# Third layer of a fused transformer block: recurrence and convolution issued among the key and value blocks instead of behind them

## The chip, the cores and the metric

The kernel runs on one core of one Trainium2 chip. The core has five engines with a queue of instructions each: TensorE (PE, matrix products; its weight loads are shown as PEld), VectorE (DVE), ScalarE (ACT), GpSimd (POOL) and SyncE (SP, which issues transfers). They meet only at semaphores. The metric is the device time of one execution in microseconds (us).

## What is computed

Four layers on 256 rows of 1024 words, all float32. The first two are attention layers, the last two a second model with key and value projections of a memory. What the change touches is the mixer of the third layer: a gated recurrence over chunks of 32 positions (four heads of 128) beside a causal depthwise convolution with 31 taps over 512 channels, followed by a layer norm and SiLU.

```python
def hgrn2_chunked(q, k, v, log_f):          # S_t = diag(f_t) S_{t-1} + k_t v_t^T, o_t = S_t^T q_t
    b = jnp.cumsum(log_f, axis=3)
    b_last = b[:, :, :, -1:, :]
    q_t = q * jnp.exp(b)
    k_t = k * jnp.exp(-b)
    scores = jnp.where(causal, jnp.einsum('bhntd,bhnsd->bhnts', q_t, k_t), 0.0)
    o_intra = jnp.einsum('bhnts,bhnsv->bhntv', scores, v)
    k_end = k * jnp.exp(b_last - b)
    d_state = jnp.einsum('bhnsd,bhnsv->bhndv', k_end, v)
    decay = jnp.exp(b_last[:, :, :, 0, :])
    ...
    return o_intra + jnp.einsum('bhntd,bhndv->bhntv', q_t, s_start)

def hybrid_ab_mixer(x, w_in, lb, hg_norm_g, cv_w, cv_b, cv_ln_g, cv_ln_b, w_out):
    q, f_pre, i_v, g, a, a_gate = jnp.split(x @ w_in, ...)
    f = lb + (1.0 - lb) * jax.nn.sigmoid(f_pre)
    k = (1.0 - lb) * jax.nn.sigmoid(-f_pre)
    o = hgrn2_chunked(q, k, i_v, jnp.log(f))
    o = o * lax.rsqrt(jnp.mean(jnp.square(o), axis=-1) + RMS_EPS) * hg_norm_g * jax.nn.silu(g)
    u = causal_depthwise_conv_31(a * jax.nn.sigmoid(a_gate), cv_w) + cv_b
    u = jax.nn.silu(layer_norm(u, cv_ln_g, cv_ln_b))
    return jnp.concatenate([o, u], axis=-1) @ w_out
```

## The kernel before, in words

**Blocks.** Every weight matrix is streamed in blocks of 1 MB (a "unit" in the code). Projections have K8 units: eight 128-row tiles of a 256-column strip; output matrices have DN units of two 128-row tiles of 1024 columns. A float32 product is made of three matmuls on a high and a low part of each operand (`passes`, L496 to L498). For each unit SyncE loads `w_raw`, which has two slots (`load`, L373, waiting for the low part of the unit two before); ScalarE copies each half to `w_hi` (`hi`, L1061, which waits for the load and for TensorE to be through with that half of the unit two before); VectorE subtracts to make `w_lo` (`lo`, L1568); TensorE waits for `lo_done` of the half it starts (`k8_unit`). So preparation runs two units ahead. After a unit ScalarE evacuates its bank in `step`, between the two high parts. A K8 unit alternates between banks 0 and 1.

**Order in the third layer** (list `PHASES`). `ab_t`, eight units: two of the convolution's input (HA), two of its gate (HG), two of the forget gate (SF and its complement SN), two of the query (HQ). `ab_nat`, four: value (HV) and output gate (GG). `xk0` and `xv0`, four each: keys and values of the cross attention that follows, from the memory; they don't depend on this layer. Then the recurrence and convolution, then `ab_out`, four DN units. Within the layer the order on every engine is written out by hand.

On VectorE the projections' stretch holds, between low parts (`stream`), the product for the convolution (UP, L2118), taps (`taps`, L2137: four operations of 128x256, one for each 128 channels, and a wait for the engine's own last step before each group), the softmax of the lower bound (L2107 to L2150), forget gate (L2155), scans (L2166), decayed keys and queries (L2178 to L2183). ScalarE makes the logarithm (L1417) and exponentials (L1420 to L1425).

**Behind the last value unit** TensorE waits for its evacuation, then does the first of six convolution taps as products with a diagonal (L935; ScalarE makes the diagonals in two buffers, L1436), turns the keys (L945), makes the scores (L950) and for seven chunks a state product (L960) and one more tap. VectorE masks the scores, updates the state after each product (L2207) and does a tap between. TensorE makes the outputs (L969, L977); then follow the sum of the convolution, the norm of the output (squares L2220, power on GpSimd, scale L2236), mean (L984) and variance (L988) of the convolution over channels by a product with ones, square root (L1451), reciprocal, SiLU (L1455), turning of the output (L994), and the splits into high and low parts (L2247, L2253). `down_phase("ab_out")` waits for all of that.

## Time and profile before

| | before |
|---|---|
| median of 3 runs | 1414.07 us (1413.47 to 1415.58) |
| profiled execution | 1414.13 us, its span 1412.3 us |
| PE busy | 1334.1 us, 94% |
| DVE busy | 856.0 us, 61% |
| ACT busy | 661.9 us, 47% |
| mean granted clock of PE | 0.967 of full speed |

Times in rows are us from the start of the span. A row of the timeline has start, duration, engine, line, operation, written tile <- read tiles, count of merged instructions, and in brackets the idle time of the engine before it with what ended it. The duration of merged instructions runs from the first start to the last end. The chain of waits lists what the end of the program followed from, each piece with its own share.

### The profile page before, as it was taken

Reading aid. Unit: us, or ns where it says so; the run is one execution under the profiler, and the core shown is the slowest. Engines: PE = TensorE matmul, PEld = TensorE weight load, DVE = VectorE, ACT = ScalarE, POOL = GpSimd, SP = SyncE. Lnnn points to the kernel's source line nnn. Section 1 sums busy time; section 2 is a strip of 40 time slices with the busy share of each in tenths; the row PEclk is TensorE's granted clock in tenths of the full one; section 3 lists DMA queues with packets and bytes.
Section 4 is the critical chain, followed back from the end, with each engine's and each line's share of the span. In section 5 each row is a group of like instructions: output and inputs, shape, how many; then the busy total and the mean of one; then the engine's idle time right before and its main releaser. Section 6 shows DMA issues by size and latency. Waiting matters only on the chain.

```text
span 1412.3 us, 23518 instructions
## 1 busy us (share of the span) xinstructions
PE 1334.1 (94%) x9430; PEld 1249.4 (88%) x9430; DVE 856.0 (61%) x1162; ACT 661.9 (47%) x1004; POOL 61.6 (4%) x72
## 2 busy tenths in 40 slices
PE   6999998999999998989996989899999999899996
PEld 6999997889998897889985888899999898799995
DVE  6566676665764444658896545655555755655555
ACT  5445676454447666345642343443433354334341
POOL 0012011000110000000000000100000000000000
PEclk9999999999999999989998999899999999899998
DMA  7555532445533332645540353665555344365552
GB/s 236 180 178 181 171 124 93 140 160 179 179 121 123 116 120 80 218 149 179 182 154 0 120 178 120 216 208 180 179 188 195 123 153 145 124 195 189 178 181 86
DMA packets 167923, 219.68 MB, mean 156 GB/s; under 512 B 3691, under 2 KB 151478, under 8 KB 167846
## 3 DMA queue, kind: packets, MB, share of 16 engines
q1 hardware_dynamic: 164502, 206.68, 45.0%
q0 software_dynamic: 3040, 11.20, 2.5%
q8 instruction: 54, 0.88, 0.3%
q10 hardware_dynamic: 304, 0.73, 0.1%
q14 instruction: 23, 0.19, 0.0%
HBM read 217.54 MB, written 1.05 MB: 155 GB/s over the span
## 4 chain that ended last, share of the span: by engine, by line
PE 83%; DVE 9%; ACT 3%; DMA 3%; issue 2%; POOL 0%; DVEq 0%; SPq 0%; ACTq 0%
PE bank L496 24%; PE bank L497 23%; PE bank L498 23%; DVE w_lo L1568 2%; PE bank L745 2%; DVE small L1592 1%; DVE h L1709 1%; PE bank L705 1%; ACT w_hi L1061 1%; PE bank L724 1%; PE bank L935 1%; DVE att L1630 1%; PE bank L757 1%; DMA w_raw<-in_o_w_out 1%; DMA w_raw<-in_e_w_mem_kv 1%
## 5 line engine op out<-in xcount | busy, mean ns | idle before, releaser
L1568 DVE TENSOR_TENSOR w_lo<-w_raw,w_hi 128x1024 fp32r<-128x1024 f32 x388 | 471.9, 1224 | 395.9 <-ACT w_hi L1061 392.5
L1061 ACT ACTIVATE w_hi<-w_raw 128x1024 fp32r<-128x1024 f32 x388 | 409.3, 1058 | 469.6 <-PE bank L498 372.5
L496 PE MATMUL bank<-u_hi,w_hi 128*128 128x256 f32 x1088 | 314.6, 289 | 3.3 <-DVE u_lo L1690 3.3
L497 PE MATMUL bank<-u_lo,w_hi 128*128 128x256 f32 x1088 | 311.6, 286 | 0.0
L498 PE MATMUL bank<-u_hi,w_lo 128*128 128x256 f32 x1088 | 311.4, 286 | 0.0
L496 PE MATMUL bank<-w_hi,y_hi 128*128 128x512 f32 (+1 forms) x656 | 235.1, 358 | 11.1 <-issue 7.6
L496 PE MATMUL bank<-w_hi,u_hi 128*128 128x256 f32 x832 | 237.9, 286 | 0.0
L497 PE MATMUL bank<-w_lo,u_hi 128*128 128x256 f32 x832 | 236.2, 284 | 0.0
L498 PE MATMUL bank<-w_hi,u_lo 128*128 128x256 f32 x832 | 236.1, 284 | 0.0
L497 PE MATMUL bank<-w_lo,y_hi 128*128 128x512 f32 (+1 forms) x656 | 231.6, 353 | 0.0
L498 PE MATMUL bank<-w_hi,y_lo 128*128 128x512 f32 (+1 forms) x656 | 231.2, 352 | 0.0
L496 PEld LDWEIGHTS bank<-u_hi,w_hi 128*128 128x128 f32 x1088 | 212.7, 196 | 6.0 <-DVE u_lo L1690 5.1
L497 PEld LDWEIGHTS bank<-u_lo,w_hi 128*128 128x128 f32 x1088 | 212.8, 196 | 0.9
L498 PEld LDWEIGHTS bank<-u_hi,w_lo 128*128 128x128 f32 x1088 | 212.6, 195 | 0.0
L497 PEld LDWEIGHTS bank<-w_lo,u_hi 128*128 128x128 f32 x832 | 160.5, 193 | 0.0
L496 PEld LDWEIGHTS bank<-w_hi,u_hi 128*128 128x128 f32 x832 | 160.5, 193 | 0.0
L498 PEld LDWEIGHTS bank<-w_hi,u_lo 128*128 128x128 f32 x832 | 160.4, 193 | 0.0
L496 PEld LDWEIGHTS bank<-w_hi,y_hi 128*128 128x128 f32 x656 | 127.4, 194 | 26.9 <-issue 9.2
L498 PEld LDWEIGHTS bank<-w_hi,y_lo 128*128 128x128 f32 x656 | 127.1, 194 | 16.2
L497 PEld LDWEIGHTS bank<-w_lo,y_hi 128*128 128x128 f32 x656 | 127.5, 194 | 14.7
L1492 POOL TENSOR_TENSOR pow_out<-pow_in,mhalf 128x1 f32<-128x1 f32 (+5 forms) x27 | 38.8, 1436 | 988.8 <-DVEq L1562 988.8
L1083 ACT ACTIVATE nat<-bank 128x512 f32<-128x512 f32 (+1 forms) x70 | 41.6, 594 | 66.5 <-PE bank L498 66.4
(277 smaller groups left out, 1323.4 us busy)
## 6 DMA issues: line engine op xcount, KB each, us to landing
w_raw<-in_e_w_in SPq DMA_DIRECT2D x28, 1024.0 KB, 5.1
w_raw<-in_o_w_in SPq DMA_DIRECT2D x28, 1024.0 KB, 5.2
w_raw<-in_ffn_wg SPq DMA_DIRECT2D x22, 1024.0 KB, 5.3
w_raw<-in_ffn_wu SPq DMA_DIRECT2D x22, 1024.0 KB, 5.3
w_raw<-in_ffn_wd SPq DMA_DIRECT2D x22, 1024.0 KB, 5.0
w_raw<-in_ab_w_in SPq DMA_DIRECT2D x12, 1024.0 KB, 5.2
w_raw<-in_e_w_out SPq DMA_DIRECT2D x8, 1024.0 KB, 4.9
w_raw<-in_o_w_out SPq DMA_DIRECT2D x8, 1024.0 KB, 5.1
```

Of the source, the lines that this page charges most:

```text
L496: pe.matmul(out_ap, ah, bh, start=start, stop=False, skip_group_check=True)
L497: pe.matmul(out_ap, ah, bl, start=False, stop=False, skip_group_check=True)
L498: return pe.matmul(out_ap, al, bh, start=False, stop=stop_, skip_group_check=True)
L705: mm = pe.matmul(bank[SC[pr]][:, SEQ * m:SEQ * m + SEQ], XQT[:, 2 * hd + j, P * m:P * m + P], (KT2 if g < 32 else KT1)[:, 2 * hd + j, :], ...
L724: mm = pe.transpose(bank[PTB][:, dst:dst + P], s[:, src:src + P], ident)
L745: mm = pe.matmul(o[:, w * m:w * m + w], p[:, SEQ * k + P * m:SEQ * k + P * m + P], v[:, k, cs], start=(k == 0), stop=(k == 1))
L757: mm = pe.transpose(bank[YTB][:, SEQ * j + P * m:SEQ * j + P * m + P], ys[g % 2][:, w * m + P * j:w * m + P * j + P], ident)
L935: mm = pe.matmul(bank[f // 2][:, SEQ * (f % 2):SEQ * (f % 2) + SEQ], DIAG[i % 2][:, P * f:P * f + P], UP[:, f, k:k + SEQ], start=(i == 0 a ...
L1061: act.activation(w_hi[:, at:at + 1024], w_raw[:, at:at + 1024], ACT.Copy).then_inc(hi_done, 1)
L1083: act.activation(dst(col), two(bank[b][:, :], SEQ), func).then_inc(evacuated, 1)
L1492: pool.tensor_tensor(pow_out[:, at:at + w], pow_in[:, at:at + w], mhalf[:, 0:w], ALU.pow)\
L1568: v.tensor_tensor(w_lo[:, at:at + 1024], w_raw[:, at:at + 1024], w_hi[:, at:at + 1024].bitcast(F32), ALU.subtract).then_inc(lo_done, 1)
```

## The change

Recurrence, convolution and norms of the third layer are issued inside and between the units of `ab_nat`, `xk0` and `xv0` (helper `among` calls `k8_unit` with `between`, a piece of work between the two halves of a unit). Part by part:

- SyncE: the first four units are ordered convolution input 0, gate 0, input 1, gate 1; ScalarE evacuates them in that order. UP is made in two halves, and taps run in two groups of 256 channels (`taps(g, n)`: n taps of group g, two operations each, and each operation waits only for the last one of its own 128 channels).
- Six taps on TensorE become two (CV_PE 6 to 2); both diagonals are made at once, both taps are done at once after state product 5. VectorE has 29 taps in place of 25.
- TensorE: keys turned within unit 1 of `ab_nat`, scores behind it, state products 0 to 6 within and behind units 2, 3 of `ab_nat` and 0, 1 of `xk0`, outputs within units 1 and 2 of `xk0`, output turned within unit 0 of `xv0`, mean within unit 2 and variance within unit 3 of `xv0`. The output phase starts its first two units when the recurrence's part is split (`hg_yl`), the other two when the convolution's part is (`conv_lo`).
- VectorE: the same steps in a new order, with single low parts (`lo_of`) between them. `two_ahead(u)` makes the two halves of unit u + 2.
- ScalarE: the forget gate's scale and shift go into the logarithm (four activations of 128x256 with scale and bias), and the key's scale is four copies of 128x256 on ScalarE; the operations of VectorE for these go. The decayed products are made in the order LF, KT, HQ.
- The softmax of the lower bound moves to the first layer's `e_kv` phase: VectorE does it before the memory keys' norm, ScalarE its exponential before the stream of `e_nat`.
- Mean, variance and the turned output use other banks (6, 7, 2 and 3).

The diff, cut to its core:

```diff
-CV_PE = 6
-PE_FIRST = 1
+CV_PE = 2
...
-            u = k8(UNIT0["ab_t"], w, 2048, 4)
+            u = UNIT0["ab_t"]
+            for j in range(2):
+                u = k8(u, w, 2048 + SEQ * j, 1)
+                u = k8(u, w, 2560 + SEQ * j, 1)
...
-            k8_phase("ab_nat", uh, ul, False)
-            pe.wait_ge(tL, turned("mem2"))
-            k8_phase("xk0", yh_[:, 8:16, :], yl_[:, 8:16, :], True)
-            k8_phase("xv0", yh_[:, 8:16, :], yl_[:, 8:16, :], False)
-            pe.wait_ge(up_ready, 1)
-            pe.wait_ge(evacuated, BANK0["xv0"] + 4)
...
+            def among(phase, j, between=None):
+
+                u, kb = UNIT0[phase] + j, BANK0[phase] + j
+                xh, xl = (uh, ul) if phase == "ab_nat" else (yh_[:, 8:16, :], yl_[:, 8:16, :])
+                k8_unit(u % 2, kb % 2, xh, xl, phase == "xk0", 2 * u + 1, kb - 1, between=between)
...
+            pe.wait_ge(tL, turned("mem2"))
+            among("ab_nat", 0)
+            among("ab_nat", 1, key_turn)
+            chunk_scores()
+            among("ab_nat", 2, lambda: state_part(0))
+            state_part(1)
+            among("ab_nat", 3, lambda: state_part(2))
+            state_part(3)
+            pe.wait_ge(up_ready, 2)
+            pe.wait_ge(hg_sm, 2)
+            among("xk0", 0, lambda: state_part(4))
+            state_part(5)
+            for i in range(CV_PE):
+                conv_tap(i)
+            among("xk0", 1, state_and_out)
+            among("xk0", 2, lambda: chunk_out(1))
+            among("xk0", 3)
+            among("xv0", 0, out_turn)
+            among("xv0", 1)
+            among("xv0", 2, conv_mean)
+            among("xv0", 3, conv_var)
             pe.wait_ge(hg_yl, 1)
+            down_phase("ab_out", 0, 2)
             pe.wait_ge(conv_lo, 2)
-            down_phase("ab_out")
+            down_phase("ab_out", 2)
...
+            act.wait_ge(lb_sub, 1)
+            act.activation(lbe, lbe, ACT.Exp).then_inc(lb_exp, 1)
             stream("e_nat", 0, 4, nat_dst(eQ))
...
-            act.activation(LF, LF, ACT.Ln).then_inc(hg_ln, 1)
-            stream("xk0", 0, 2, t_dst(KT2))
+            act.wait_ge(evacuated, BANK0["ab_t"] + 6)
+            for f in range(4):
+                ins = act.activation(LF[:, f, :], SF[:, f, :], ACT.Ln, scale=oml[:, f:f + 1], bias=lb[:, f:f + 1])
+            ins.then_inc(hg_ln, 1)
+            step(UNIT0["ab_t"] + 6, copy_out(t_dst(HQ), 0), BANK0["ab_t"] + 6)
             act.wait_ge(hg_b, 1)
             act.activation(SF, HB, ACT.Exp)
             act.activation(KT, HB, ACT.Exp, scale=-1.0)
...
+            for f in range(4):
+                ins = act.activation(SN[:, f, :], SN[:, f, :], ACT.Copy, scale=oml[:, f:f + 1])
             act.wait_ge(hg_b, 2)
             act.activation(LF, LF, ACT.Exp).then_inc(hg_e, 1)
...
+                            v.wait_ge(dve_step, tap_step[f])
                             mark(v.scalar_tensor_tensor(CA[:, f, :], UP[:, f, k:k + SEQ], ws, CA[:, f, :],
                                                         ALU.mult, ALU.add))
...
+            mark(v.memset(UP, 0.0))
+            up(0)
+            taps(0, 2)
+            two_ahead(tu + 2, lambda: taps(0, 2))
+            taps(0, 1)
+            two_ahead(tu + 3, lambda: taps(0, 2))
+            up(1)
+            two_ahead(tu + 4, lambda: taps(1, 2))
+            taps(1, 2)
+            two_ahead(tu + 5, lambda: taps(1, 2))
+            taps(1, 2)
+            scans()
+            two_ahead(tu + 6, lambda: taps(1, 1))
+            taps(0, 1)
+            decayed()
+            two_ahead(tu + 7)
+            taps(1, 2)
+            two_ahead(nu, lambda: taps(0, 2))
+            taps(1, 2)
+            two_ahead(nu + 1, lambda: taps(0, 1))
+            masked_scores()
+            state(0)
...
+            state(6)
+            two_ahead(ku + 1, lambda: taps(0, 3), lambda: taps(1, 3))
+            two_ahead(ku + 2, lambda: taps(0, 4), lambda: taps(1, 3))
+            out_squares()
+            lo_of(ku + 5, 0)
+            out_norm()
+            lo_of(ku + 5, 1)
+            taps(0, 2)
+            two_ahead(vu, lambda: taps(1, 4))
+            taps(0, 2)
+            lo_of(vu + 3, 0)
+            y_low()
+            taps(0, CV_K)
+            lo_of(vu + 3, 1)
+            taps(1, CV_K)
+            conv_sum()
+            lo_of(vu + 4, 0)
             v.wait_ge(cv_mu, 1)
```

`tu`, `nu`, `ku`, `vu` are the first units of `ab_t`, `ab_nat`, `xk0`, `xv0`. Between `state(0)` and `state(6)` VectorE alternates: half a low part, two taps of a group, the next state; `gate_scale` and one tap stand before `state(6)`.

## Rows read from the trace of the kernel before

**Rows 1.** The page: engines' busy time; loads (last: us to landing).

```profile
PE 1334.1 (94%) x9430; PEld 1249.4 (88%) x9430; DVE 856.0 (61%) x1162; ACT 661.9 (47%) x1004; POOL 61.6 (4%) x72
...
w_raw<-in_ab_w_in SPq DMA_DIRECT2D x12, 1024.0 KB, 5.2
```

**Rows 2.** By stretch: length; busy PE, PEld, DVE, ACT, POOL; clock; DMA.

```profile
680.00:727.70 47.70, 47.01 (x392) 46.81 (x391) 41.60 (x62) 27.81 (x33) 0.00 (x0) 1.00 0.56 188
727.70:777.00 49.30, 35.05 (x224) 29.23 (x224) 35.48 (x72) 16.73 (x39) 2.77 (x3) 0.89 0.08 29
```

**Rows 3.** The chain of waits, start of the output phase.

```profile
777.33 0.76 PE bank L496
...
778.10 0.43 PE bank L497
...
788.92 0.23 PE bank L498
```

**Rows 4.** Timeline of TensorE behind the last value block.

```profile
726.73 0.28 PE L498 MATMUL bank<-w_hi,y_lo 128*128 128x256 f32 x1
...
730.02 1.97 PE L935 MATMUL bank<-att 128*128 128x256 f32 x8 [3.00 <-ACT att L1436]
731.82 1.03 PE L945 MATMUL bank<-cst,nat 128*128 128x128 f32 x8
732.69 1.95 PE L950 MATMUL bank<-nat 128*128 128x128 f32 x16
...
749.62 1.71 PE L960 MATMUL bank<-nat 32*128 32x128 f32 x16
...
751.25 1.16 PE L969 MATMUL bank<-nat 128*128 128x128 f32 x8
...
754.26 1.16 PE L969 MATMUL bank<-nat 128*128 128x128 f32 x8
...
757.75 1.99 PE L984 MATMUL bank<-att,ones 128*128 128x256 f32 x8
```

**Rows 5.** Timeline of VectorE in the third layer; the taps' line (mean ns).

```profile
625.07 1.23 DVE L1568 TENSOR_TENSOR w_lo<-w_raw,w_hi 128x1024 fp32r<-128x1024 f32 x1
...
645.28 1.67 DVE L2137 SCALAR_TENSOR_TENSOR att<-att,gT 128x256 f32<-128x256 f32 x4
...
649.62 3.38 DVE L2137 SCALAR_TENSOR_TENSOR att<-att,gT 128x256 f32<-128x256 f32 x8
...
684.92 2.44 DVE L2166 TENSOR_TENSOR_SCAN nat<-cst,nat 128x256 f32<-128x256 f32 x4 [1.15 <-ACT nat L1417]
...
688.88 2.36 DVE L1568 TENSOR_TENSOR w_lo<-w_raw,w_hi 128x1024 fp32r<-128x1024 f32 x2
...
738.77 1.12 DVE L2207 SCALAR_TENSOR_TENSOR nat<-nat,small,bank 128x128 f32<-128x128 f32 x4 [0.62 <-PE bank L960]
...
758.48 1.23 DVE L2220 TENSOR_TENSOR nat<-nat 128x1024 f32<-128x1024 f32 x1 [4.13 <-ACT nat L1449]
...
L2137 DVE SCALAR_TENSOR_TENSOR att<-att,gT 128x256 f32<-128x256 f32 x96 | 40.1, 481 | 0.3
```

**Rows 6.** ScalarE: block 8's evacuation; two forms (busy, mean ns).

```profile
663.69 0.60 ACT L1083 ACTIVATE nat<-bank 128x512 f32<-128x512 f32 x1 [1.74 <-PE bank L498]
...
L1204 ACT ACT_TABLE_LOAD x7 | 9.0, 1283 | 0.1
...
L1204 ACT ACTIVATE att<-att,small 128x256 f32<-128x256 f32 x12 | 6.0, 496 | 0.0
```

**Rows 7.** Timeline of VectorE: the lower bound's last steps.

```profile
664.65 0.17 DVE L2150 TENSOR_SCALAR small<-small 128x4 f32<-128x4 f32 x1
```

**Rows 8.** Timelines of VectorE and ScalarE in the first layer.

```profile
52.75 3.50 DVE L1568 TENSOR_TENSOR w_lo<-w_raw,w_hi 128x1024 fp32r<-128x1024 f32 x3 [0.32 <-DVE nat L1666]
...
55.13 0.60 ACT L1083 ACTIVATE nat<-bank 128x512 f32 x1 [1.93 <-PE bank L498]
```

**Rows 9.** Timeline of TensorE before the third layer.

```profile
602.68 1.97 PE L604 MATMUL bank<-cst,h 128*128 128x128 f32 x8 [2.80 <-DVEq L2095]
```

More of the change, by code:

```diff
@@ L952, in _, with conv_tap @@
-            mm.then_inc(hg_st, 1)
-            pe.wait_ge(hg_kn, 1)
-            for n in range(N_CHUNK - 1):
+            def conv_tap(i):
+                pe.wait_ge(diag_ready, i + 1)
+                k = CV_K - CV_PE + i
+                for f in range(4):
+                    mm = pe.matmul(bank[4 + f // 2][:, SEQ * (f % 2):SEQ * (f % 2) + SEQ],
+                                   DIAG[i % 2][:, P * f:P * f + P], UP[:, f, k:k + SEQ],
+                                   start=(i == 0 and f % 2 == 0), stop=(i == CV_PE - 1), skip_group_check=True)
+                mm.then_inc(diag_used, 1)
@@ L996, in _, with out_turn, conv_mean @@
-            mm.then_inc(hg_yt, 1)
+            def out_turn():
+                pe.wait_ge(hg_y, 1)
+                for f in range(4):
+                    for m in range(2):
+                        mm = pe.transpose(bank[2 + f // 2][:, SEQ * (f % 2) + P * m:SEQ * (f % 2) + P * m + P],
+                                          ON[:, m, P * f:P * f + P], ident)
+                mm.then_inc(hg_yt, 1)
+            def conv_mean():
+                pe.wait_ge(conv_ready, 2)
+                for f in range(4):
+                    mm = pe.matmul(bank[6][:, 0:SEQ], ones[:, :], CA[:, f, :], start=(f == 0), stop=(f == 3))
+                mm.then_inc(cv_mu, 1)
@@ new lines, in conv_var @@
+            def conv_var():
+                pe.wait_ge(cv_c, 2)
+                for f in range(4):
+                    mm = pe.matmul(bank[7][:, 0:SEQ], ones[:, :], CS[:, f, :], start=(f == 0), stop=(f == 3))
+                mm.then_inc(cv_var, 1)
+            def among(phase, j, between=None):
+                u, kb = UNIT0[phase] + j, BANK0[phase] + j
+                xh, xl = (uh, ul) if phase == "ab_nat" else (yh_[:, 8:16, :], yl_[:, 8:16, :])
+                k8_unit(u % 2, kb % 2, xh, xl, phase == "xk0", 2 * u + 1, kb - 1, between=between)
@@ L2194, in _, with two_ahead @@
-            v.wait_ge(hg_tr, 1)
-            for m in range(2):
-                v.tensor_tensor(STM[:, m, :].rearrange("p (a b) -> p a b", b=P),
-                                bank[4 + m][:, :].rearrange("p (a b) -> p a b", b=P), hm, ALU.mult).then_inc(hg_sm, 1)
-            for n in range(N_CHUNK - 1):
+                        tap_step[f] = steps[0]
+            def two_ahead(u, first=None, second=None):
+                lo_of(u + 2, 0)
+                if first is not None:
+                    first()
+                lo_of(u + 2, 1)
+                if second is not None:
+                    second()
@@ new lines, in _ @@
+            masked_scores()
+            state(0)
+            lo_of(nu + 4, 0)
+            taps(0, 2)
+            state(1)
+            lo_of(nu + 4, 1)
+            taps(1, 2)
+            state(2)
+            lo_of(nu + 5, 0)
+            taps(0, 2)
+            state(3)
+            lo_of(nu + 5, 1)
+            taps(1, 2)
+            state(4)
+            lo_of(ku + 2, 0)
+            taps(0, 2)
+            state(5)
+            lo_of(ku + 2, 1)
+            gate_scale()
+            taps(1, 1)
```

328 lines of the change are left out of this document (155 added, 173 removed).

## Prediction

> **What bounds the kernel now.** I read the page's busy shares first: TensorE is busy 94% of the span, so outside its pauses there is nothing to win. VectorE has 61% [rows 1]. Then the busy time of two stretches of the third layer: in the later half of the projections TensorE is full (47.01 of 47.70 us) and VectorE is busy 87%; in the next, which holds recurrence, convolution and norms with no projection beside them, the two share the time, 35 us each of 49.3, and the clock is 0.89 [rows 2]. So this layer is serial there. The chain of waits shows that the output phase's first matmul starts at 777.33 [rows 3]. TensorE's timeline shows where the stretch begins: its last value matmul starts at 726.73 and runs 0.28, so it ends at 727.0; a pause of 3.0 behind ScalarE's diagonals, then dense work of 27 us up to the mean at 757.75, and from VectorE's squares at 758.48 on a relay of short steps on three engines [rows 4, 5]. Hence 777.3 - 727.0 = 50.3 us without weight matmuls. After it the output phase begins at the lower clock, 1.2 GHz: a 128x512 matmul takes 0.43 of the chain at 778.10 against 0.23 at 788.92 [rows 3]. Thirteen such steps (to 783.2) lose 13 x 0.2 = 2.65 us.
>
> **What moves on TensorE.** Its records in that stretch price every item at full clock [rows 4]: key transposes 0.9, scores 1.8, seven state products, two in 1.63 (749.62 to 751.25) to 1.1 each with a wait (I take 1.0), a tap 1.95, outputs of the first four chunks 3.0 (751.25 to 754.26), of the last four 3.5 (to 757.75), a mean 1.9, a variance of the same eight matmuls as much, turning the output as much as the eight key transposes, 1.0. Six taps become two, so 4 x 1.95 = 7.8 us are gone. The rest is inserted: 0.9 + 1.8 + 7.0 + 3.9 + 6.5 + 3.8 + 1.0 = 24.9 us. If nothing waited, the last value block would end at 727.0 + 24.9 = 751.9, and the output phase start there: a gain of 25.4, with the clock 28.1 us. This is the floor.
>
> **What VectorE must do in that time.** Prices are start-to-start [rows 5]: a half block's low part 1.14 (two last 2.36, one 1.23), a large product as much or 1.25 with a wait, scans and subtraction 3.96 (684.92 to 688.88), a state 1.07, squares and sum 2.7 (two of 1.23, a small one and their waits), mean, difference and square 3.1 by the same count. A tap of four operations lasts 1.67 with single ones of 0.48, so they start 0.397 apart; eight last 3.38, so the first of a group, which waits for the last of the group before, starts 0.52 after it. The new taps run in pairs and wait for the operation two back, which has ended: I take 0.397 x 2 = 0.795 per pair-tap. 29 taps x 2 pairs = 58 x 0.795 = 46.1 us, against 25 x 1.71 = 42.8 before. Forget-gate scaling and key scaling (1.38 + 1.14) go to ScalarE. From the low part of block 4 to the sum of the convolution: 32 low parts 36.5, taps 46.1, zeroing and two products 2.4, scans 4.0, decayed products 3.6, scores 1.3, states 7.1, gate 1.2, squares 2.7, norm 2.5, low part of the output 1.2, sum 1.4: 110 us. Starting at 626.2 (the low part at 625.07 [rows 5]) this can't be done before 736.2, and the mean on TensorE needs it.
> The rows above have taps of 0.48 starting 0.397 apart without a wait and 0.52 with one [rows 5]. The Trainium skill, "VectorE: DVE Perf Modes", section "The DRAIN you can't avoid", says that the next operation does not start before the pipe has emptied (unless it is one that isn't held back) and that a semaphore between operations costs nothing extra. By that rule taps would start 0.48 apart, grouped or not, the tail below would end 26 x 0.083 = 2.2 us later and the time be 1400; I go by the rows.
>
> **The walk.** Number the blocks from 0 (eight of the first projection, four of the gate and value one, four keys, four values, then 20 to 23 output). Block 8 is evacuated at 663.69 now [rows 6], every block takes 5.76, and ScalarE's and VectorE's preparation of a block's half runs two blocks ahead of it.
> *Block 9.* ScalarE now makes the logarithm in four pieces of 128x256, then exponentials, then four scalings. A 128x256 one takes 0.50, four with overlap an estimated 1.6, and a table load 1.28 [rows 6]; a pass over 1024 words takes 1.05, 0.95 where the next follows. Block 5 is evacuated three blocks before 8, at 646.4; its two copies and the high part end at 648.45; table and logarithm at 651.4; scans on VectorE to 655.4; table and exponentials to 657.4; scalings 659.0; last exponential 660.05. VectorE's three products end at 663.65 (the last also waits for block 7's late evacuation, 661.6), and only then comes the low part of block 9, at 664.85. TensorE is ready at 663.5: it waits 1.4 us, a wait that the kernel now hasn't.
> *Blocks 9 to 14.* With the inserts TensorE ends them at 671.8, 680.4, 688.3, 696.3, 711.2, 720.5. At each of them VectorE has its state, low parts and taps done in time: for block 13 it is even through at 701.6 and waits until 705.3 for the last state product, and for ScalarE's copies until 712.8 and 722.0. A load takes 5.2 us from issue (page's median [rows 1]) and is issued when the low part two blocks before is made; all land before they are wanted.
> *From 722.0 on VectorE sets the time.* Seven low parts 8.0, 13 pair-taps 10.3, squares 2.7, norm with the power on GpSimd 2.9, output's low part 1.2, sum 1.4: 26.5, so the convolution's sum is there at 748.7. The norm is ready at 732.4 while TensorE stands in the middle of block 16 at 729.2: a wait of 3.2. The mean is wanted in the middle of block 18 at 744.9: a wait of 3.8. Behind it lie the mean 1.9, half a block 2.9, block 19 5.8 and the variance 1.9: the output phase starts at 761.2. The last convolution steps (square root, reciprocal, normalising, SiLU, split) then take from 758.4 to about 768, beside blocks 20 and 21, which need 10.9 us to 772: hidden, 4 us to spare.
> *The sum.* 777.3 - 761.2 = 16.1, plus 2.65 for the clock of the output phase. **Clock of the two new pauses:** before, the pause of 3.0 us to 730.02 left the clock high (a tap of 1.97 like all later ones), one of 2.8 before 602.68 did not: eight transposes took 1.97 there against 1.03 at 731.82 [rows 4, 9]. So a pause of 3 to 4 us may cost nothing or some 2.7 (the mean at 3.8 in place of 1.9 and a part of a half block). The first pause's loss would vanish in the second. I take 2.0.
> **Bound preparation moved forward.** The softmax of the lower bound (six small operations and an exponential) leaves this layer and stands before the first layer's key norm on VectorE. Its first two took 0.4, the four after the exponential 0.8, the last at 664.65 [rows 7]; with the exchange with ScalarE 1.6 us. There three low parts start at 52.75, the first ends at 53.98, and the block before the one that wants it is evacuated at 55.13, TensorE being free at 54.9 [rows 8]: 0.9 of the 1.6 is covered and 0.7 is not. Nearest bounds 0 and 1.6. The next load is late by as much, but its low part at 63.08 has 2 us to spare. ScalarE waits there until 47.1 in place of starting its copy at 46.38: nobody needs that copy before 52.75.
> Order of the first loads, half of the first product early, and the output phase in two calls: nothing, TensorE is full over all of them.
> In all 16.1 + 2.65 - 2.0 - 0.7 = 16.1 us. The profiled execution took 1414.13 (its span of 1412.3 and 1.8 around it), the median of the runs is 1414.07: **1398 us**.
>
> **Rivals.** *(a) TensorE stays the bound.* If VectorE's idle stretches near 703 to 722 fill, that is if ScalarE and the states come earlier than walked, both pauses (7.0) and block 9's 1.4 shrink: 1386 to 1391. For it: VectorE's bare work ends at 736. Against: the waits follow from the written order, and taps can't pass a state. 0.17.
> *(b) The preparation falls behind.* Low parts stand behind up to four taps (3.2 us) and behind states that wait for TensorE; each may make TensorE wait at blocks 9 to 17, where I found one wait. Six of 1 us and both clock losses (2.7 each): 1398 + 6 + 3 = 1407; range 1404 to 1411. For it: VectorE is at 87% already among the key and value blocks [rows 2]. 0.20.
> *(c) Slower.* The loop low part, load (5.2), copy, low part again closes around VectorE's queue: a late low part makes the next load late. Its price is one wait per block; it turns the balance when the twelve blocks 8 to 19 lose 16/12 = 1.35 us each beyond my walk; at 2 us each 1422. Against: 5.2 + 2.2 + 3.2 = 10.6 us of loop against 15.3 for two blocks. 0.03.
> *(d) The change doesn't overlap:* a semaphore of the recurrence always comes last, and TensorE stands inside a block as long as it stood behind them; only the four taps (7.8) are gained, and partly lost: about 1412, the same. 0.03.
>
> **Numbers.** Forecast 1391 to 1404: 0.57. With (a) 0.17, (b) 0.20, (c) 0.03, (d) 0.03. What this kernel's runs can tell from no change is about 0.2%, 2.8 us. Faster 0.93, same 0.04, slower 0.03. The range, 1388 to 1408, leaves out the ends of (a) and (b), with (c) and (d).
>
> **What would show it.** Between the last value matmul and the first output matmul no pause; the first output matmuls at 0.23; TensorE's waits in the layer: about 1.4 before block 9, 3 before turning the output, 4 before the mean, each behind VectorE; taps 0.397 apart; VectorE over 85% busy from 630 to 750; TensorE some 0.7 late near 55. Wrong: a mean without a wait (then rival a), waits on low parts in several blocks (b), a pause before the third output block on the convolution's split.

## The result and the profile after

The changed kernel takes 1399.05 us in the median of four runs (1398.35 to 1399.62), the kernel before 1413.77 beside it (1413.39 to 1415.58): a ratio of 0.9896, 95% interval 0.9881 to 0.991, 14.7 us less. The forecast was 1398. The profiled execution of the changed kernel has a span of 1397.8 us, 14.5 less than before, and a mean granted clock of 0.969.

Its page, the line of busy times, answers to [rows 1]: TensorE has 7.7 us less work (four taps gone), VectorE 3.2 more.

```profile
PE 1326.4 (95%) x9398; PEld 1244.5 (89%) x9398; DVE 859.2 (61%) x1171; ACT 656.6 (47%) x994; POOL 61.5 (4%) x72
```

**Where the time went.** GpSimd makes the powers of the norms ahead of the third layer and behind it, with the same code in both kernels, so its rows are good marks for the length of the layer. Timeline of GpSimd, kernel before (start, duration, line, operation, idle time ahead of it):

```profile
591.67 0.56 POOL L1492 TENSOR_TENSOR pow_out<-pow_in,mhalf 128x1 f32<-128x1 f32 x1 [1.29 <-DVEq L1562]
...
802.57 0.57 POOL L1492 TENSOR_TENSOR pow_out<-pow_in,mhalf 128x1 f32<-128x1 f32 x1 [25.80 <-DVEq L1562]
```

The same, kernel after:

```profile
594.10 0.55 POOL L1553 TENSOR_TENSOR pow_out<-pow_in,mhalf 128x1 f32<-128x1 f32 x1 [1.30 <-DVEq L1623]
...
788.11 0.57 POOL L1553 TENSOR_TENSOR pow_out<-pow_in,mhalf 128x1 f32<-128x1 f32 x1 [37.45 <-DVEq L1623]
```

The layer shrinks from 210.90 to 194.01 us, by 16.9. Of that 2.4 are lost before it begins (594.10 against 591.67), and behind it nothing moves: the second mark is 14.46 earlier, the span 14.5 shorter. "The layer" below is always the distance between these two marks; the times of the prediction's walk have to be read 2.4 later. Blocks are numbered as in the walk, and "the norm" and "the mean" stand for TensorE's turning of the output, which waits for the norm, and for its product that makes the convolution's mean.

The waits view of TensorE from 600 to 800, kernel after (who waited for whom: total us, times, longest):

```profile
PE bank L983 <- DVEq L1623: 3.6, 1, 3.6
PE bank L606 <- DVEq L2174: 2.8, 1, 2.8
PE bank L991 <- DVEq L1623: 2.3, 1, 2.3
PE bank L498 <- DVE w_lo L1629: 1.5, 1, 1.5
...
```

L606 is the turning of the input that [rows 9] shows before (2.80); two waits of 0.7 and 0.6 on the layer's input follow in the view. The other three are new and are the three pauses of the walk: ahead of turning the output (L983), of the mean (L991) and of block 9 (L498). The stretches in which they lie (length; busy PE, PEld, DVE, ACT, POOL; clock), kernel after:

```profile
680.00:727.70 47.70, 47.70 (x388) 44.99 (x388) 37.71 (x82) 15.98 (x19) 0.00 (x0) 1.00 0.34 111
727.70:755.00 27.30, 21.34 (x152) 20.78 (x151) 25.18 (x40) 9.05 (x12) 2.76 (x3) 0.87 0.50 158
755.00:765.00 10.00, 10.00 (x78) 9.74 (x77) 6.13 (x6) 4.36 (x5) 0.00 (x0) 1.00 0.50 181
```

Against [rows 2]: there TensorE was busy 35.05 of 49.30 us, with no weights to multiply. Now the stretch that holds the norm's and the mean's pause is 27.3 us with 21.3 busy, blocks of weights among them. There VectorE is busy 92% (25.18) and TensorE waits for it; in the ten us behind it TensorE is full.

The chain of waits, kernel after, where the output phase begins (the last matmul of 256 columns, then those of 512):

```profile
765.70 0.12 PE bank L500
765.82 0.23 PE bank L498
766.06 0.23 PE bank L499
```

It begins without a pause and at 2.4 GHz, where [rows 3] shows 0.43 a step.

### The profile page after: what moved, and what is told of

Its sections match the earlier page's. It is cut to its first block, busy times and chain, and to the rows that moved or that the text cites. A ratio compares the mean times of both kernels' runs of the same rounds, so it can differ in the third digit from the quotient of the medians.

```text
span 1397.8 us, 23384 instructions
## 1 busy us (share of the span) xinstructions
PE 1326.4 (95%) x9398; PEld 1244.5 (89%) x9398; DVE 859.2 (61%) x1171; ACT 656.6 (47%) x994; POOL 61.5 (4%) x72
## 3 DMA queue, kind: packets, MB, share of 16 engines
HBM read 217.54 MB, written 1.05 MB: 156 GB/s over the span
## 4 chain that ended last, share of the span: by engine, by line
PE 80%; DVE 11%; ACT 4%; DMA 3%; issue 2%; POOL 0%; DVEq 0%; SPq 0%; ACTq 0%
PE bank L498 23%; PE bank L499 23%; PE bank L500 23%; DVE w_lo L1629 3%; PE bank L747 2%; DVE small L1653 1%; ACT w_hi L1098 1%; DVE h L1770 1%; PE bank L707 1%; PE bank L726 1%; DVE att L1691 1%; PE bank L759 1%; DMA w_raw<-in_o_w_out 1%; DMA w_raw<-in_e_w_mem_kv 1%; PE bank L666 1%
## 5 line engine op out<-in xcount | busy, mean ns | idle before, releaser
L498 PE MATMUL bank<-u_hi,w_hi 128*128 128x256 f32 x1088 | 314.7, 289 | 3.3 <-DVE u_lo L1751 3.3
L498 PE MATMUL bank<-w_hi,u_hi 128*128 128x256 f32 x832 | 239.1, 287 | 2.2 <-DVE w_lo L1629 2.2
L498 PE MATMUL bank<-w_hi,y_hi 128*128 128x512 f32 (+1 forms) x656 | 235.3, 359 | 3.7 <-DVE w_lo L1629 3.7
L498 PEld LDWEIGHTS bank<-u_hi,w_hi 128*128 128x128 f32 x1088 | 213.0, 196 | 6.0 <-DVE u_lo L1751 5.1
L498 PEld LDWEIGHTS bank<-w_hi,u_hi 128*128 128x128 f32 x832 | 160.9, 193 | 3.0 <-DVE w_lo L1629 2.6
L498 PEld LDWEIGHTS bank<-w_hi,y_hi 128*128 128x128 f32 x656 | 127.8, 195 | 19.1 <-DVE w_lo L1629 3.0
L499 PEld LDWEIGHTS bank<-w_lo,y_hi 128*128 128x128 f32 x656 | 127.8, 195 | 14.5
```

Of the source, the lines that this page charges most:

```text
L498: pe.matmul(out_ap, ah, bh, start=start, stop=False, skip_group_check=True)
L499: pe.matmul(out_ap, ah, bl, start=False, stop=False, skip_group_check=True)
```

## The experiments

Theory A is the prediction's account, with the sizes of this trace: TensorE is full except in three pauses, each of which follows from a place in VectorE's written order; a pause can also halve the clock. The expectations name its rivals by letters. All twelve kernels start from the changed kernel unless said otherwise. A pair-tap is one tap of one group of 256 channels, two operations. The kernel before took 1415.54, 1413.83 and 1414.1 beside the three groups of runs (1415.54 beside norm_first, filled, block9_first and one_tap), and each ratio is to the one beside it, so across groups ratios or layers compare better than times.

### The order decides, not the work: norm_first, filled

```diff
-            two_ahead(ku + 2, lambda: taps(0, 4), lambda: taps(1, 3))
+            two_ahead(ku + 2, lambda: taps(0, 4))
             out_squares()
             lo_of(ku + 5, 0)
             out_norm()
             lo_of(ku + 5, 1)
+            taps(1, 3)
             taps(0, 2)
```

> The changed kernel with one edit on VectorE: the three taps of the second group that stood before the output's squares stand behind its norm. TensorE's pause before turning the output was 3.6 us with 3.5 us at the lower clock behind it, the pause before the mean 2.3 us. Theory A (from block 14 on VectorE's queue alone sets the end; its sum of work is unchanged): the first pause falls to about 1.2 us and its low clock goes, but the mean's pause grows by that to about 6 us and may lose the clock itself, so the output phase starts no earlier: 1398 to 1402 us. Rival B (each pause costs its own length): 2.4 us and the low clock's 1.9 us are won, 1395 us.

Measured 1400.34 (1398.3 to 1401.33), ratio 0.9898, 0.988 to 0.9917. Waits view of TensorE, 600 to 800:

```profile
PE bank L991 <- DVEq L1623: 6.2, 1, 6.2
...
PE bank L498 <- DVE w_lo L1629: 1.5, 1, 1.5
...
PE bank L983 <- DVEq L1623: 1.2, 1, 1.2
...
```

Three pair-taps moved behind the norm take 2.4 us off the norm's pause (3 x 0.79) and put 3.9 onto the mean's, since TensorE now comes to the mean earlier, without the pause's last 2.4 us and the 2.6 of lost clock behind it, while VectorE has as much to do as before and is there only 1.1 earlier. Nothing is won: both steps wait for one queue, and what is postponed falls due at the mean. The layer is 1.5 longer (195.48), for the mean now runs at half the clock, as its line shows (durations min/median/max in ns; 379 in the changed kernel):

```profile
L991 PE MATMUL bank<-att,ones x8: 634/634/795, 751.4 to 754.6; 128*128 128x256 f32 x8
```

The second kernel brings those three pair-taps forward instead, and three of the other group that stood between norm and mean, into VectorE's idle stretches before state 6 and behind it:

```diff
-            taps(1, 1)
+            taps(1, 4)
             state(6)
-            two_ahead(ku + 1, lambda: taps(0, 3), lambda: taps(1, 3))
-            two_ahead(ku + 2, lambda: taps(0, 4), lambda: taps(1, 3))
+            two_ahead(ku + 1, lambda: taps(0, 6), lambda: taps(1, 3))
+            two_ahead(ku + 2, lambda: taps(0, 4))
             out_squares()
             lo_of(ku + 5, 0)
             out_norm()
             lo_of(ku + 5, 1)
-            taps(0, 2)
```

> The changed kernel with six taps of a pair of channel blocks moved forward on VectorE into its two idle stretches: three before the last state, three before the wait for the high part of block 15's second half. Nothing is added or left out. Theory A (VectorE's queue behind block 14 sets the end): the norm is 2.4 us and the convolution's sum 4.8 us earlier, TensorE's first pause about 1 us at full clock, the mean's pause 1 to 2 us; 1394 us (1392.5 to 1396). Rival C (the pauses follow from TensorE's order and from ScalarE's copies, not from VectorE's work): no change, 1399 us.

Measured 1392.26 (1388.58 to 1397.66), ratio 0.9845, 0.9819 to 0.987; the layer takes 188.35, 5.7 less, of which 0.9 lies at its input, ahead of all that the edit touches (last section). The norm's pause is 1.2, and the transposes behind it run at full clock (272 ns). The idle time of VectorE before state 6 was 3.42 in the changed kernel and is 1.05 here (its timeline, behind the eight operations of four pair-taps):

```profile
702.83 3.25 DVE L2209 SCALAR_TENSOR_TENSOR att<-att,gT 128x256 f32<-128x256 f32 x8
707.12 1.12 DVE L2261 SCALAR_TENSOR_TENSOR nat<-nat,small,bank 128x128 f32<-128x128 f32 x4 [1.05 <-PE bank L957]
```

The mean's pause is 2.3 as in the changed kernel, and both edits leave 1.2 of the norm's. A expected the gain and about 1 us at the norm, the 3.6 less three pair-taps; C expected none. That no further tap can shorten this rest, A did not say.

### The floor under the pauses: taps_out

```diff
-                    if k >= CV_K - CV_PE:
+                    if k >= 15:
                         return
```

> The changed kernel with only 15 of the 29 taps on VectorE; 14 taps of both groups (28 x 0.8 = 22 us of VectorE) are left out, so the convolution's result is not the reference's. Nothing else is moved. Theory A: the pauses before the output's turning (3.6 and its low clock) and before the mean (2.3) go and block 9's 1.5 stays: 1391 us (1390 to 1392.5), no less, because behind them TensorE is full. Rival F (every us of VectorE's work stands on the path): 1399 - 22 = 1377 us. Rival C (the pauses have another cause): 1399 us.

Measured 1392.25 (1389.69 to 1393.54), ratio 0.9844, 0.9825 to 0.9862; layer 188.01. The kernel leaves out 28 pair-taps, 22 us of VectorE's work, and pauses of 1.5, 1.2 and 1.3 remain. A said that the norm's and the mean's would go: its time is met, its pauses are not. F, by which every us of VectorE counts (1377), is out. The timeline of VectorE shows what the pauses are made of:

```profile
736.32 1.23 DVE L1629 TENSOR_TENSOR w_lo<-w_raw,w_hi 128x1024 fp32r<-128x1024 f32 x1 [3.19 <-ACT w_hi L1098]
...
742.08 1.23 DVE L1629 TENSOR_TENSOR w_lo<-w_raw,w_hi 128x1024 fp32r<-128x1024 f32 x1 [0.88 <-ACT w_hi L1098]
743.23 1.28 DVE L2307 TENSOR_TENSOR att<-att,bank 128x512 f32<-128x512 f32 x2
```

and ScalarE's, where the copy that this low part needs follows the evacuation, and that the end of a block on TensorE:

```profile
740.51 0.60 ACT L1120 ACTIVATE mkv<-bank 128x512 f32<-128x512 f32 x1 [0.79 <-PE bank L500]
741.00 1.05 ACT L1098 ACTIVATE w_hi<-w_raw 128x1024 fp32r<-128x1024 f32 x1
```

The convolution's sum (L2307) stands in the queue behind a low part that can't start until the block ended on TensorE, 0.6 us of evacuation and 1.05 of copy are over: block end 740.5, low part 742.1 to 743.3, sum to 744.5, mean 744.6; but half a block is done on TensorE in 2.9. So TensorE waits 1.3 even if VectorE has nothing else to do. In filled the 2.3 are this floor, with one pair-tap (0.98) behind the same low part, which has waited 0.62 there. In the changed kernel that low part starts without a wait (749.96): the queue's work is later than the floor. Of its 3.6 and 2.3 the taps thus make 2.4 and 1.0, and 1.2 and 1.3 would remain without them. The norm's floor is of the same kind: in norm_first the squares start at 725.51, behind a low part at 724.37 that has waited 1.31 for its copy. Block 9 is no matter of taps either: its low part stands behind products that wait for ScalarE, not behind taps, and keeps its 1.5.

### Block 9: block9_first

```diff
             taps(0, 1)
+            lo_of(tu + 9, 0)
             decayed()
-            two_ahead(tu + 7)
+            lo_of(tu + 9, 1)
```

> The changed kernel with the low part of block 9's first half before the three decayed products on VectorE instead of behind them. It took TensorE 1.5 us of waiting at block 9 before. Theory A: TensorE's clock sets VectorE's last anchor at block 14, so what is won at block 9 reaches the end: the wait falls from 1.5 to 0, the second half's low part comes up to 0.7 late; 1397.5 to 1398.5 us. Rival D (what TensorE gains early is given back at the mean, because VectorE's sum of work sets all): 1399 us, with the mean's pause longer by 1 us or more.

Measured 1398.71 (1393.92 to 1401.15), ratio 0.9876, 0.9852 to 0.9901. The pause before block 9 is gone from the view, and the mean's grew only from 2.3 to 2.5, where D had it longer by 1 or more. The layer is 192.51, 1.5 less, but 0.7 of that lies at its input, ahead of the edit (last section). Behind it two differences of the clock nearly cancel: the mean lost the clock (634 ns a matmul), and the clock behind the norm's pause was back sooner (1.00 from 739 on). The median of the runs shows 0.3, within the spread. So that the pause went is shown; what it is worth in time is not.

### All pauses out: reordered

Both edits, and low parts put behind the steps that TensorE waits for:

```diff
+            lo_of(tu + 9, 0)
             decayed()
-            two_ahead(tu + 7)
+            lo_of(tu + 9, 1)
...
-            taps(1, 1)
+            taps(1, 5)
             state(6)
-            two_ahead(ku + 1, lambda: taps(0, 3), lambda: taps(1, 3))
-            two_ahead(ku + 2, lambda: taps(0, 4), lambda: taps(1, 3))
+            two_ahead(ku + 1, lambda: taps(0, 6), lambda: taps(1, 3))
+            lo_of(ku + 4, 0)
+            taps(0, 4)
             out_squares()
+            lo_of(ku + 4, 1)
             lo_of(ku + 5, 0)
             out_norm()
             lo_of(ku + 5, 1)
-            taps(0, 2)
...
             lo_of(vu + 3, 0)
-            y_low()
             taps(0, CV_K)
-            lo_of(vu + 3, 1)
             taps(1, CV_K)
             conv_sum()
+            y_low()
+            lo_of(vu + 3, 1)
```

> The changed kernel with its whole work in another order on VectorE: the low part of block 9 before the decayed products, seven taps of a pair in VectorE's idle stretches before the last state and before block 15's second half, the output's squares before the low part of block 16's second half, the convolution's sum before the low parts that stood ahead of it. Theory A (VectorE's queue sets TensorE's pauses): all four pauses (1.5, 3.6 with its low clock, 2.3) go; 1387 us (1385.5 to 1389), and TensorE has no pause over 0.5 us from the first weight block of the layer to the output phase. Rival C (TensorE's and ScalarE's order make the pauses): as the kernel with only the taps moved, 1392 us.

Measured 1388.75 (1386.08 to 1390.18), ratio 0.9815, 0.9796 to 0.9833: 10 us less than the changed kernel. The layer takes 183.42, 10.6 less. In the waits view neither L983, L991 nor L498 on a weight's low part is left (the other rows are of the layers' input, ahead of the third layer and behind it), and the mean runs at full clock:

```profile
PE bank L606 <- DVE u_lo L1751: 4.6, 2, 3.9
PE bank L606 <- DVEq L2174: 2.8, 1, 2.8
PE bank L498 <- DVE u_lo L1751: 1.1, 2, 0.6
```

```profile
L991 PE MATMUL bank<-att,ones x8: 377/379/379, 742.9 to 744.4; 128*128 128x256 f32 x8
```

The three pauses were 7.4 us and the clock lost behind the norm's 2.6 (worked out below); 0.3 of the rest lies at the layer's input. No work was removed for it.

### The two new conditions ahead of the output phase: mean_behind, wait_all

```diff
-            among("xv0", 2, conv_mean)
-            among("xv0", 3, conv_var)
+            among("xv0", 2)
+            among("xv0", 3)
+            conv_mean()
+            conv_var()
```

> The changed kernel with one part undone: mean and variance of the convolution are issued on TensorE behind the last value block instead of inside the last two. Theory A: the pause before the mean (2.3) is covered by the blocks, but TensorE then waits for VectorE's 3.1 us between mean and variance with nothing to do, and the copies behind the last block wait for the variance; the output phase starts 1 to 3 us later: 1401 us (1399.5 to 1404). Rival G (it is the place of the mean that costs, not its time): 1396.7 us, faster by the pause.

Measured 1401.72 (1399.89 to 1403.6), ratio 0.9907, 0.9887 to 0.9928; layer 196.44, 2.4 more. The mean's pause is gone, but between mean and variance TensorE now has nothing to do while VectorE subtracts and squares:

```profile
763.53 2.81 PE L998 MATMUL bank<-att,ones 128*128 128x256 f32 x7 [3.15 <-DVE att L2375]
```

(Seven of the eight; 634 ns each in the median.) That is 3.1 of pause and half the clock in place of 2.3 at full clock. The last value blocks are cover for VectorE's 3 us, and worth it even at the price of a pause.

```diff
             pe.wait_ge(hg_yl, 1)
+            pe.wait_ge(conv_lo, 2)
             down_phase("ab_out", 0, 2)
-            pe.wait_ge(conv_lo, 2)
             down_phase("ab_out", 2)
```

> The changed kernel with the output phase held until the convolution's part is split too, instead of starting its first two blocks when the recurrence's part is. The split ended 7.1 us after the output phase began. Theory A (the convolution's last steps are hidden under blocks 20 and 21): a pause of 7.1 us, and behind it the lower clock as in the kernel before, 2.6 us: 1408.7 us (1406 to 1410). Rival J (what is hidden there is small, since the steps would be earlier with nothing beside them): below 1404 us.

Measured 1409.94 (1404.81 to 1411.28, nine runs), ratio 0.9969, 0.9957 to 0.9982; layer 204.01, 10.0 more. Timeline of TensorE, then the chain of waits:

```profile
773.98 0.77 PE L498 MATMUL bank<-w_hi,y_hi 128*128 128x512 f32 x1 [7.06 <-issue]
```

```profile
774.75 0.43 PE bank L499
...
779.44 0.43 PE bank L498
779.87 0.35 PE bank L499
780.22 0.23 PE bank L500
```

7.1 us of pause and 13 steps at 1.2 GHz, the same lost clock as at the start of the output phase in [rows 3]. So with all else in place the split of the output phase, one line of the change, holds 10 of the 15 us: the last steps of the convolution lie beside blocks 20 and 21.

### Four taps fewer on TensorE: old_two_taps, one_tap

In the kernel before:

```diff
-CV_PE = 6
+CV_PE = 2
```

> The kernel before with the count of taps alone changed: two on TensorE in place of six, 29 on VectorE in place of 25, everything in its old order behind the value blocks. TensorE loses 7.8 us, VectorE gains four taps, 6.5 us. Theory A (there both engines set the pace in turn: a tap and a state product took TensorE 3.0 us, a state and a tap VectorE 2.7): the states go by 0.3 us faster each, but the taps left for the end take VectorE 6.5 us, of which its waits of 3.4 us and the outputs on TensorE cover most: 1414 to 1417 us, no gain. Rival I (the four taps on TensorE were a gain of their own): 1414 - 7.8 = 1406 us.

Measured 1415.31 (1412.01 to 1417.4, ten runs), ratio 1.0005, 0.9994 to 1.0015: nothing. From the waits view of TensorE, 700 to 780:

```profile
PE bank L496 <- issue: 8.0, 1, 8.0
PE bank L988 <- DVE att L2232: 4.7, 1, 4.7
PE bank L960 <- DVE nat L2207: 3.2, 4, 1.5
```

TensorE loses its 7.8 us of taps and gets 3.2 us of waits for the states (L960), since VectorE has the taps to do between states. The clock of the stretch (727 to 777) falls from 0.89 to 0.79, by my estimate worth 50 x 0.10 = 5 us more. A had the time, but not this part of the clock. The saving of taps is none of its own; it exists only where TensorE has weights to multiply meanwhile. In the changed kernel one more tap can be moved:

```diff
-CV_PE = 2
+CV_PE = 1
```

> The changed kernel with one convolution tap on TensorE in place of two: TensorE has 1.95 us less between blocks 12 and 13, VectorE four operations of 0.4 us more, at the end of its taps. Theory A (VectorE is anchored to TensorE's block 14 and sets the time from there): 1.95 us won before block 14, 1.6 us lost behind it: 1398.7 us, the pause before the mean 1.6 us longer. Rival E (TensorE's work alone sets the end): 1397 us. Rival D (VectorE's sum of work sets all): 1400.6 us.

Measured 1399.88 (1395.34 to 1402.61), ratio 0.9892, 0.9869 to 0.9914. TensorE saves 1.95, VectorE has two pair-taps more and the mean's pause grows by as much, from 2.3 to 3.9. By that the time should stand; the layer is 2.0 longer (195.96), since the mean falls to half the clock (634 ns a matmul). Pause as A had it, sign not: the clock made the difference, which A had not priced here. The times alone can't tell A (1398.7) from D (1400.6).

### The taps' start-to-start time: each_waits

```diff
                         else:
-                            v.wait_ge(dve_step, tap_step[f])
+                            wait_own()
```

Each tap operation then waits for the last one on the engine, not for the last one of its own channels.

> The changed kernel with a wait for the operation just before in front of every tap operation, in place of the wait for the last one on the same channels. The work is the same. Theory A (such a wait makes the start-to-start time 0.52 us in place of 0.397): the 26 tap operations behind block 14 take 3.2 us more, the pause before the mean grows from 2.3 to 5 to 6 us, that before turning the output by 0.7: 1402.5 us (1401 to 1405). By the Trainium skill, VectorE: DVE Perf Modes, The DRAIN you can't avoid, a semaphore between operations costs nothing extra: 1399 us, taps at one distance in both.

Measured 1403.72 (1402.42 to 1405.01), ratio 0.9931, 0.9915 to 0.9947; layer 199.17, 5.2 more. Eight operations in a row, timeline of VectorE, the changed kernel and this one:

```profile
740.08 3.25 DVE L2209 SCALAR_TENSOR_TENSOR att<-att,gT 128x256 f32<-128x256 f32 x8
```

```profile
740.90 4.13 DVE L2209 SCALAR_TENSOR_TENSOR att<-att,gT 128x256 f32<-128x256 f32 x8
```

(3.25 - 0.48) / 7 = 0.396 apart without the wait, (4.13 - 0.48) / 7 = 0.52 with it: 0.12 us for a wait on the operation just before. The pauses grow to 4.3, 4.1 and 1.7. The Trainium skill, "VectorE: DVE Perf Modes", section "The DRAIN you can't avoid", says that a semaphore between operations costs nothing extra. Here the measurement decides against it: the operations of 0.48 us overlap unless one waits for the one just before.

### The lower bound in the first layer: bound_later, reordered_bound_later

The softmax's VectorE part moved behind the memory keys' norm, its exponential on ScalarE behind the stream (the block of L2049 to L2066 moves whole):

```diff
             done(mkn_ready)
             stream("e_nat", 0, 4)
+            lp = gT[:, GCOL["lb_param_2"]:GCOL["lb_param_2"] + 12].rearrange("p (w k) -> p k w", k=4)
...
+            stream("e_nat", 0, 4, nat_dst(eQ))
             act.wait_ge(lb_sub, 1)
             act.activation(lbe, lbe, ACT.Exp).then_inc(lb_exp, 1)
-            stream("e_nat", 0, 4, nat_dst(eQ))
```

> The changed kernel with the softmax of the lower bound four blocks later in the first layer (behind the memory keys' norm and four low parts of blocks instead of before them). Theory A: the 0.7 to 0.9 us that TensorE stood there by my sum go, and are seen at the first norm of the queries near 87 us of the span; 1398.2 us. Rival H (that delay is covered, or repaid by later pauses before the third layer): 1399 us.

Waits view of TensorE from 20 to 120, the changed kernel, then this one:

```profile
PE bank L595 <- DVE u_lo L1739: 2.4, 1, 2.4
PE bank L595 <- DVE att L1675: 1.6, 1, 1.6
PE bank L498 <- DVE w_lo L1629: 0.7, 1, 0.7
```

```profile
PE bank L595 <- DVE u_lo L1739: 2.8, 1, 2.8
PE bank L595 <- DVE att L1675: 2.3, 1, 2.3
```

The wait of 0.7 on a low part is gone; the kernel before has none either in this window. But TensorE's waits in it sum to 3.6 there, 4.7 in the changed kernel and 5.1 here, so the window shows no net gain. The time is 1396.52 (1396.27 to 1398.62), ratio 0.9876, 0.9856 to 0.9895: 2.5 less than the changed kernel, more than 0.7, while the layer itself came out 1.25 longer. So neither A (1398.2) nor H (1399) has the time: 3.0 us were gained ahead of the layer, where unchanged code varies by more (last section), and what the move of the softmax is worth stays open. Combined with the order above:

> The reordered kernel (all its edits) with the softmax of the lower bound four blocks later in the first layer as well. The reordered kernel took 1388.75 us, without a pause in the third layer; in the first layer it still has one of 0.7 us behind the low part that the softmax delays. That goes: 1388.0 us, between 1386 and 1389.5; the pause of 0.7 isn't in the trace. If the delay is repaid before the third layer by pauses that shift, 1388.75 us.

Measured 1387.72 (1386.79 to 1390.0), ratio 0.9815, 0.9801 to 0.9828. The wait of 0.7, which reordered still has, is gone here, but the time is not to be told apart from reordered's (1388.75; layer 183.79 against 183.42). Both are 10 to 11 us faster than the changed kernel and 25 to 26 faster than the one before.

## Why the prediction was right, and where it was not

**The frame held.** That VectorE sets the time from the last keys to the mean, that TensorE is full outside three pauses, that the output phase starts in full clock and hides the end of the convolution (its split, L2385, ends at 772.8; the blocks over it at about 776.6): each is in the rows above. Layer: 16.9 won, 16.75 predicted (16.1 + 2.65 - 2.0). At the lower bound TensorE waits 0.7, as predicted, at 56.41; that this costs 0.7 of the whole is not shown, for 2.4 are lost ahead of the layer. old_two_taps and wait_all show the two halves of the mechanism: without overlap the fewer taps give nothing, and with the overlap, but one wait for the whole output, 10 of the 15 us are gone.

**The pauses.** Predicted 1.4, 3.2 and 3.8, measured 1.5, 3.6 and 2.3. Block 9 is as walked: VectorE waits 0.58 for the logarithm before the scans, 0.49 for the last exponential, and only then makes the low part; block9_first takes the pause away. The four pieces of the logarithm took 2.08 where 1.6 was estimated, the four scalings 1.70. VectorE idles where the walk has it: 3.42 before state 6 (3.7 walked), 3.02 and 1.32 before the low parts of blocks 15 and 16 (2.9 and 1.35 by the walk's prices). Taps stand 0.396 apart, VectorE is busy 88% from 630 to 750 (105.3 of 120).

**The clock, the step that failed.** I wrote that a loss in the first pause would vanish in the second, and took the 2.0 us at the mean. In the profiled execution it was lost at the first pause and not at the mean. Turning the output right behind the pause of 3.6, timeline of TensorE (1.03 for the same eight in [rows 4]), and three stretches of its clock:

```profile
736.19 1.97 PE L983 MATMUL bank<-cst,nat 128*128 128x128 f32 x8 [3.62 <-DVEq L1623]
```

```profile
733.00:737.00 4.00, 0.81 (x4) 0.81 (x5) 3.39 (x4) 0.72 (x1) 0.56 (x1) 0.70 0.00 0
737.00:741.00 4.00, 4.00 (x21) 4.00 (x20) 4.00 (x9) 0.00 (x0) 0.00 (x0) 0.50 0.57 186
741.00:745.00 4.00, 4.00 (x34) 4.00 (x34) 3.22 (x7) 1.54 (x2) 0.00 (x0) 0.95 0.23 76
```

From 736.2 to 745 that is 0.8 x 0.5 + 4 x 0.5 + 4 x 0.05 = 2.6 us of TensorE's work. How much of it vanished, bound_later shows, which has the same code here. There the clock outlived the same pause of 3.6 and fell at the mean, behind a pause of 3.8: the place and the length that I had given (durations in ns):

```profile
L983 PE MATMUL bank<-cst,nat x8: 272/272/328, 732.7 to 733.5; 128*128 128x128 f32 x8
```

```profile
L991 PE MATMUL bank<-att,ones x8: 634/634/796, 749.1 to 752.2; 128*128 128x256 f32 x8
```

So most of the 2.6 did vanish: the mean's pause is 2.3 in place of 3.8. The rest did not, because TensorE in turn makes VectorE late: block 16's end is late, so ScalarE's copy, and so the next low part, which waits 0.78 in the changed kernel and not at all in bound_later:

```profile
744.12 1.22 DVE L1629 TENSOR_TENSOR w_lo<-w_raw,w_hi 128x1024 fp32r<-128x1024 f32 x1 [0.78 <-ACT w_hi L1098]
```

**The walk.** For the tail I had 26.5 us of VectorE with nothing between (722.0 + 26.5 is 748.5; I wrote 748.7). It missed this 0.78 and some 0.4 of small gaps, and began 1.1 us too early (the low part at 725.55, walked 722.0 + 2.4). That 1.1 grew over blocks 9 to 14. Blocks 10, 11 and 12, walked to 682.8, 690.7 and 698.7 (with the 2.4), end at 683.3, 691.6 and 699.9, since half a block beside an insert takes 3.06 us, where the walk has 2.88, half of 5.76. Timeline of TensorE, the first matmul of such a half and the state products behind it:

```profile
684.40 0.38 PE L498 MATMUL bank<-w_hi,u_hi 128*128 128x256 f32 x1
...
687.46 1.15 PE L957 MATMUL bank<-nat 32*128 32x128 f32 x8
```

So the convolution's sum ends at 753.4 where 748.7 + 2.4 = 751.1 was walked, 2.3 late, and the output phase starts at 765.82 where 763.6 was: 2.2 late. The 2.0 that I took for the clock at the mean covers that in size, not in place: that the layer's sum comes out within 0.2 us is luck.

**What the rivals had.** (a), that TensorE stays the bound, did not happen in this kernel, but its number, 1386 to 1391, is what reordered reaches: VectorE's idle time before state 6 was the room, and the written order kept the taps out of it. The argument against (a), that taps can't pass a state, was right for this kernel. (b): no further low part kept TensorE waiting in blocks 10 to 19, and with it (c) fell. (The 15.3 us for two blocks in (c) are in none of its rows; two bare blocks take 11.5, so its margin was smaller than it says.) (d): the output phase starts 11.5 us earlier (765.82 against 777.33), more than the taps' 7.8. What I had not seen is the floor that taps_out shows: I put the pauses down to the sum of VectorE's work, while 2.5 of the 5.9 us at norm and mean remain without the taps, for a low part that waits for a copy stands in front of the step that TensorE waits for.

## To carry to other kernels

Work moved among blocks of weights is hidden only as far as its steps come early enough in every in-order queue: list for each wait of the full engine what stands ahead of its releaser, and put steps that wait for that engine's own progress (here the low part of the next block) behind the releaser, not ahead. Look for idle time of the second engine a few blocks before a pause and bring forward work that depends on nothing; work moved later than the pause only moves the pause. When a phase needs two inputs that come at different times, give its first blocks the wait that they need and no more.

## What was not expected of the hardware

**The time ahead of an unchanged stretch.** Code up to the first mark is the same in nine of the kernels above and the changed one, yet the mark lies between 591.24 (taps_out) and 595.32 (wait_all) in their profiled executions. It begins with the input: VectorE's first norm waits for it in the changed kernel,

```profile
17.66 2.47 DVE L1653 BATCH_NORM_STATS2 small<-h 128x6 f32<-128x512 f32 x4 [1.20 <-DMA h<-in_x]
```

and starts at 16.25 in the kernel before. Later the distance between before and after goes back to 0.06 (237.90 against 237.84 on GpSimd) and out again to 2.4. The waits of bound_later from 20 to 120 (2.8 and 2.3 where the changed kernel has 2.4 and 1.6) are of that kind. Why is open. An edit worth under 2 us can't be judged here by the whole time. The length of its own layer is better, but not free of this either: from the mark to the first transposes among its blocks (621.09) the changed kernel takes 26.99, filled 26.12, block9_first 26.26, bound_later 26.42 and the others made from it 26.73 to 27.06, with the same code. In filled, block9_first and bound_later the clock outlived the layer's first pause, timeline of TensorE in filled ([rows 9] has 1.97 for the same eight):

```profile
604.40 1.09 PE L606 MATMUL bank<-cst,h 128*128 128x128 f32 x8 [2.82 <-DVEq L2174]
```

**A pause keeps or loses the clock, and its length alone doesn't say which.** The same code shows both: the 2.8 ahead of the layer's first transposes lost it in the kernel before, in the changed one and in nine of the twelve (eight transposes in 1.97), and kept it in filled, block9_first and bound_later (1.09), which then lost it at a pause of only 1.2 that followed; the norm's 3.6 lost it in the changed kernel (421 ns a matmul) and kept it in bound_later (272). Besides these it was kept behind the mean's 2.3 (379 ns a matmul) and before the 3.0 to 730.02 [rows 4], and lost at 2.5 (the mean in block9_first, 634 ns), 3.1 (mean_behind), 3.8 (bound_later), 3.9, 4.1, 6.2 and 7.1; in each_waits it fell within the transposes behind 4.3 (272 to 421 ns). A loss cost 2.6 us of TensorE's work where I worked it out (behind the norm's pause, and 13 steps of 0.2 in wait_all), but only about 1.5 behind the norm's pause of block9_first, where the clock was back by 739. What decides was not tried.
